# Retrieved experts of a two-block network on one Trainium2 core: u and v rows fetched by one gather from a joined table, dots and mixing in one pass, top-k head by head

## What is computed

```
# per block of 128 tokens (there are two); 8 heads, 128 keys in each of two halves, 16384 experts
q = (hb @ w_q).reshape(tb, 8, 2, 128)
scores = einsum("thpc,hpnc->thpn", q, keys)
s_top, i_top = top_k(scores, 16)                    # 16 best of 128, per head and half
cand = s_top[..., 0, :, None] + s_top[..., 1, None, :]   # 256 sums per head
best, pos = top_k(cand, 16)                         # 16 best of 256
idx = the two key numbers of pos, as 128 * i + j    # 128 experts per token
gate = softmax(best)
u = take(expert_u, idx)                             # [token, 128, 1024]
act = gelu(einsum("tkd,td->tk", u, hb))
vv = take(expert_v, idx)
out = einsum("tk,tkd->td", gate * act, vv)
```

## Time and profile before

| what | us |
|---|---|
| median of 3 timed runs | 3087.06 (3086.28 to 3093.58) |
| span of the profiled execution, first to last instruction | 3081.3 |
| PE / DVE / ACT / POOL busy in it | 2539.9 / 1885.4 / 1017.9 / 549.8 |
| first gather issued, last gather issued | 2268.65, 3058.88 |

### The profile page before, as it was taken

The page is one execution under the profiler, slowest core; times in us unless marked ns, Lnnn a source line. Parts: engine busy times, 40 slices in busy tenths (PEclk is TensorE's granted clock), DMA queues, the critical chain, the costliest instruction groups (busy, mean ns, idle before and its releaser), DMA issues.

```text
span 3081.3 us, 31757 instructions
## 1 busy us (share of the span) xinstructions
PE 2539.9 (82%) x11382; PEld 1991.5 (65%) x11382; DVE 1885.4 (61%) x2532; ACT 1017.9 (33%) x952; POOL 549.8 (18%) x664
## 2 busy tenths in 40 slices
PE   8998999999899999999999979899950067800687
PEld 7777998767788888888888868688850023300233
DVE  5333544431798898888888853534188875388422
ACT  2212331111577686676766731115010000000000
POOL 0000000000000000000000000000036667666775
PEclk9999999999899999999999989999975589955899
DMA  6323554430699999999999953134339998899997
GB/s 220 132 88 96 185 172 154 137 109 25 249 355 353 334 369 338 354 350 338 353 352 333 374 210 118 65 110 172 116 133 370 358 338 302 322 372 364 343 332 266
DMA packets 316765, 775.01 MB, mean 252 GB/s; under 512 B 17850, under 2 KB 59528, under 8 KB 316680
## 3 DMA queue, kind: packets, MB, share of 16 engines
q1 hardware_dynamic: 240996, 503.54, 46.0%
q0 software_dynamic: 73728, 268.47, 24.0%
q10 hardware_dynamic: 1956, 1.86, 0.2%
HBM read 772.76 MB, written 1.05 MB: 251 GB/s over the span
## 4 chain that ended last, share of the span: by engine, by line
PE 73%; POOL 10%; issue 8%; DVE 5%; DMA 2%; ACT 1%; POOLq 1%; DVEq 0%; ACTq 0%
PE banks L498 15%; PE banks L659 12%; PE banks L661 12%; PE banks L660 12%; POOL dense_weights L1236 9%; PE banks L546 5%; PE banks L1007 3%; PE banks L622 2%; PE banks L626 2%; PE banks L459 2%; DMA dense_weights<-in_peer_v,gather_stage 2%; POOL gather_stage L1229 1%; PE banks L816 1%; PE banks L745 1%; PE banks L772 1%
## 5 line engine op out<-in xcount | busy, mean ns | idle before, releaser
L1894 DVE TENSOR_TENSOR expert_tiles_low<-expert_tiles,expert_tiles_high 128x2048 fp32r<-128x2048 f32 x336 | 752.5, 2284 | 90.0 <-ACT expert_tiles_high L1447 89.8
L1007 PE MATMUL banks<-dense_weights,work 128*128 128x512 f32 x768 | 351.0, 614 | 413.7 <-DVE work L2246 206.9
L1447 ACT ACTIVATE expert_tiles_high<-expert_tiles 128x2048 fp32r<-128x2048 f32 x336 | 624.6, 1911 | 66.4 <-DMA expert_tiles<-in_moe_w_down 52.7
L1007 PEld LDWEIGHTS banks<-dense_weights,work 128*128 128x128 f32 x768 | 147.7, 197 | 615.8 <-issue 606.1
L659 PE MATMUL banks<-expert_tiles_high,gathered_parts 128*128 128x512 f32 x896 | 355.4, 397 | 2.2 <-DVE gathered_parts L1903 2.2
L661 PE MATMUL banks<-expert_tiles_high,gathered_parts 128*128 128x512 f32 x896 | 350.5, 391 | 0.0
L660 PE MATMUL banks<-expert_tiles_low,gathered_parts 128*128 128x512 f32 x896 | 349.9, 390 | 0.0
L1209 POOL MEMSET work<- 64x1024 f32 x1 | 0.9, 944 | 1839.4 <-DVE normed L1638 1839.4
L2220 DVE CUSTOM_DVE_ANT_0 dense_weights<-dense_weights,banks 128x1024 f32<-128x1024 f32 x256 | 296.5, 1216 | 50.6 <-DMA dense_weights<-in_peer_u,gather_stage 49.7
L498 PE MATMUL banks<-normed,dense_weights 128*128 128x256 f32 x1280 | 281.3, 382 | 7.1 <-DVE normed L1638 7.1
L1236 POOL DMA_INDIRECT dense_weights<-in_peer_v,gather_stage x256 | 259.5, 1014 | 114.0 <-issue 80.1
(11 more groups left out here) (353 smaller groups left out, 3414.4 us busy)
## 6 DMA issues: line engine op xcount, KB each, us to landing
expert_tiles<-in_moe_w_gate SPq DMA_DIRECT2D x112, 1024.0 KB, 5.1
expert_tiles<-in_moe_w_up SPq DMA_DIRECT2D x112, 1024.0 KB, 5.2
expert_tiles<-in_moe_w_down SPq DMA_DIRECT2D x112, 1024.0 KB, 4.9
dense_weights<-in_w_in SPq DMA_DIRECT2D x12, 2048.0 KB, 7.8
dense_weights<-in_w_xkv SPq DMA_DIRECT2D x8, 2048.0 KB, 8.0
dense_weights<-in_w_in SPq DMA_DIRECT2D x10, 1280.0 KB, 13.8
expert_tiles<-in_ffn_w_gate SPq DMA_DIRECT2D x11, 1024.0 KB, 5.3
expert_tiles<-in_ffn_w_up SPq DMA_DIRECT2D x11, 1024.0 KB, 5.3
```

The source lines that it names most:

```text
L1007: mm = pe.matmul(halves[half], diag[:, q, j, :], gathered_rows[:, q * BATCH + j, half * 512:(half + 1) * 512], start=False, stop=False)
L1447: act.activation(high_tile(j), raw_tile(j), ACT.Copy).then_inc(g.high, 1)
L1894: dve.tensor_tensor(low_tile(j), raw_tile(j), high_tile(j).bitcast(F32), ALU.subtract).then_inc(g.split, 1)
```

## The change

The host hands over one table `peer_rows`, whose row e is u[e] followed by v[e], 8 KB. One gather fetches both rows of a slot (128 rows of 8 KB, 1.05 MB), so there are 256 gathers and not 512. A batch is now two slots (2.1 MB, as before), and there are seven batch buffers: two lie in memory that the first block used, one in the slot of the key weights and four in the slots of the four `pq` weight tiles (`G.pair_at`), and each can be filled when PE is done with what was in it (`G.pair_freed`).

For every batch n of 128, in one pass: DVE makes two dots (`products`), ACT takes gelu of the two, DVE makes two diagonals from `gelu x gate` (`weights`, one tensor_scalar each, run after the dots of the next batch), PE mixes both rows (`mix`, four matmuls of 512 columns) and frees the buffer. DVE's own share of the mixing and the four phases are gone. Top-k is done head by head (`choose`, 16 units), two heads ahead of the gathers, between the batches. POOL reads the indices where they lie, without the staging copy. The loops are written out, not run as loops.

```diff
+PAIR_ROWS = 2
+PAIR_BUFS = 7
+AHEAD_UNITS = 2
+EARLY, LATE = 3, 4
...
+                def mix(b, halves, first, last):
+                    for n in range(b * BLOCK_BATCHES + first, b * BLOCK_BATCHES + last):
+                        pe.wait_ge(diag_ready, n + 1)
...
+                        for j in range(PAIR_ROWS):
+                            for half in range(2):
+                                mm = pe.matmul(halves[half], diag[(n * PAIR_ROWS + j) % 8], pair_rows(n)[:, j, 1, half * 512:(half + 1) * 512],
+                                               start=False, stop=end and j == PAIR_ROWS - 1)
+                        mm.then_inc(mix_done, 1)
...
+                G.pair_at = [RING, RING + 1] + [(keys_at + i) % RING for i in range(RING)]
+                for g in range(4):
+                    linear(("pq", g), "a", 1, x, KT)
+                    scores(0, g)
+                    if g == 0:
+                        tokens("v", 0)
+                    elif g == 1:
+                        first = out_banks("v", 0)
+                    elif g == 2:
+                        mix(0, first, 0, EARLY)
+                G.pair_freed = [None, None] + G.freed[keys_at:]
...
+                mix(0, first, EARLY, BLOCK_BATCHES)
+                second = out_banks("a", 1)
+                mix(1, second, 0, BLOCK_BATCHES)
...
+            for n in range(TB * BLOCK_BATCHES):
+                if n % HEAD_BATCHES == 0:
+                    pool.wait_ge(index_ready, n // HEAD_BATCHES + 1)
+                if n >= PAIR_BUFS:
+                    pool.wait_ge(mix_done, n - PAIR_BUFS + 1)
+                elif G.pair_freed[n]:
+                    pool.wait_ge(*G.pair_freed[n])
+                for j in range(PAIR_ROWS):
...
+                    pool.indirect_dma_start(out=pair_rows(n)[:, j, :, :].rearrange("p t d -> p (t d)"), out_offset=None,
+                                            in_=t["peer_rows"], in_offset=bass.IndirectOffsetOnAxis(ap=rows_at[:, c:c + 1], axis=0)
+                                            ).then_inc(gathered[n % PAIR_BUFS], 16)
...
+                for g in range(4):
                     copies(("pq", g), qP[:, 4 * g:4 * g + 4, :], 2)
...
+                    scores(0, g)
+                    if g == 1:
+                        for u in range(AHEAD_UNITS):
+                            share(u)
+                    elif g == 2:
+                        activations(0, EARLY)
...
+            def choose(u):
+                b, h = divmod(u, PHEADS)
+                dve.wait_ge(act_took, G.took["key_scores", b, h // 2])
+                top16(key_top, key_at, key_scores[b][:, 2 * h:2 * h + 2, :], key_rest, 2)
...
+                def products(n):
+                    dve.wait_ge(gathered[n % PAIR_BUFS], 16 * PAIR_ROWS * (n // PAIR_BUFS + 1))
+                    for j in range(PAIR_ROWS):
+                        u_row, c = pair_rows(n)[:, j, 0, :], n * PAIR_ROWS + j
+                        ins = dve.tensor_tensor_reduce(u_row, u_row, tokens(b), 1.0, 0.0, ALU.mult, ALU.add, dots[:, c:c + 1])
+                    ins.then_inc(dot_done, 1)
...
+                def weights(n):
+                    dve.wait_ge(act_ready, n + 1)
+                    if n >= 4:
+                        dve.wait_ge(mix_done, n - 3)
+                    for j in range(PAIR_ROWS):
+                        c = n * PAIR_ROWS + j
+                        ins = dve.tensor_scalar(diag[c % 8], ident[:, :], acts[:, c:c + 1], gates[:, c // TOPK, c % TOPK:c % TOPK + 1],
+                                                ALU.mult, ALU.mult)
+                    ins.then_inc(diag_ready, 1)
...
+                for u in range(AHEAD_UNITS):
+                    choose(u)
+                for n in range(TB * BLOCK_BATCHES):
+                    u, part = divmod(n, HEAD_BATCHES)
+                    products(n)
+                    if n:
+                        weights(n - 1)
+                    if part == 0:
+                        normalise(u)
+                    elif part == HEAD_BATCHES // 2 - 1 and u + AHEAD_UNITS < UNITS:
+                        choose(u + AHEAD_UNITS)
```

More of the change, by code:

```diff
@@ L337, in two_blocks @@
[L337 to L351, removed]
+        key_scores = [view(6144 + 2048 * b, 2 * PHEADS, PK) for b in range(TB)]
+        diag = [view(10240 + P * i, P) for i in range(8)]
+        key_rest, pairs_, pairs_rest = view(11264, 2, PK), view(11520, 1, TOPK * TOPK), view(11776, 1, TOPK * TOPK)
@@ L1010, in peer @@
-                    pe.wait_ge(zero_ready, 1)
-                    for half in range(2):
-                        G.end(pe.matmul(halves[half], ones[0:1, :], zero_row, start=False, stop=True), ("out", b, half))
+                    return halves
+                def mix(b, halves, first, last):
+                    for n in range(b * BLOCK_BATCHES + first, b * BLOCK_BATCHES + last):
+                        pe.wait_ge(diag_ready, n + 1)
+                        end = n == (b + 1) * BLOCK_BATCHES - 1
+                        for j in range(PAIR_ROWS):
+                            for half in range(2):
+                                mm = pe.matmul(halves[half], diag[(n * PAIR_ROWS + j) % 8], pair_rows(n)[:, j, 1, half * 512:(half + 1) * 512],
+                                               start=False, stop=end and j == PAIR_ROWS - 1)
+                        mm.then_inc(mix_done, 1)
@@ L1582, in scores, with share, activations @@
                     ready(("key_scores", b, g))
[L1583 to L1592 removed]
+                    take(act.activation(key_scores[b][:, 4 * g:4 * g + 4, :], pair(banks_of(("key_scores", b, g)), 4, P), ACT.Copy))
+                def share(u):
+                    act.wait_ge(margin_ready, u + 1)
+                    act.activation(gates[:, u, :], gates[:, u, :], ACT.Exp, accum_out=gate_sum[:, u:u + 1]).then_inc(margin_exp, 1)
+                def activations(first, last):
+                    for n in range(first, last):
+                        act.wait_ge(dot_done, n + 1)
+                        s = slice(n * PAIR_ROWS, (n + 1) * PAIR_ROWS)
+                        act.activation(acts[:, s], dots[:, s], ACT.Gelu).then_inc(act_ready, 1)
+                        if n % HEAD_BATCHES == HEAD_BATCHES - 2 and n // HEAD_BATCHES + AHEAD_UNITS < UNITS:
+                            share(n // HEAD_BATCHES + AHEAD_UNITS)
                 def final(b):
[L1595 to L1596 removed]
+                    act.wait_ge(mix_done, (b + 1) * BLOCK_BATCHES)
+                    n = (0 if b == 0 else 4) + (G.took["out", b, 0] - 1) % 4
+                    step.now(act.activation(final_sq, psum_all[:, n:n + 2, :].rearrange("p h d -> p (h d)"), ACT.Square,
+                                            accum_out=final_ss[:, b:b + 1]))
                     act.activation(final_std[:, b:b + 1], final_ss[:, b:b + 1], ACT.Sqrt, bias=EPS_AP, scale=1.0 / D).then_inc(final_std_ready, 1)
@@ L2265, in finish @@
                 def finish(b):
[L2267 to L2270 removed]
+                    dve.wait_ge(mix_done, (b + 1) * BLOCK_BATCHES)
+                    n = (0 if b == 0 else 4) + (G.took["out", b, 0] - 1) % 4
                     dve.wait_ge(final_std_ready, b + 1)
@@ L2316 @@
     arrays, t = {}, {}
-    for name, a in inputs.items():
+    rows = _np.concatenate([inputs["peer_u_2"][0], inputs["peer_v_2"][0]], axis=1)
+    laid = {name: a for name, a in inputs.items() if name not in ("peer_u_2", "peer_v_2")} | {"peer_rows": rows}
+    for name, a in laid.items():
         a = _np.ascontiguousarray(a)
```

273 lines of the change are left out of this document (66 added, 207 removed).

## The result

The changed kernel takes 2934.43 us (median of 4 runs, 2931.72 to 2938.63), the kernel before 3089.63 us on the same chip (3086.28 to 3093.58). The ratio is 0.949, with a 95% interval of 0.948 to 0.951: 155 us less. 3006 us was forecast, with a range from 2965 to 3060.

What follows compares the result with a forecast made beforehand. DMA was taken to bound the gather stream, with POOL's pace almost on top. Batch 6 at 2288.1, plus 2.2, 695.4 and 14.8, gave a span of 3000.5, 80.8 less than before: 3006 us, range 2965 to 3060.

Steps and rivals of the forecast that it cites:

- The pace of DMA: Steady gather stream: DMA's own pace read as 375 GB/s in the dot phase, 358 in mixing; 5.70 us per batch taken.
- the rival built on it: Gather stream: 8 KB rows flow faster, at 401 GB/s or 5.23 us a batch, giving 2949 us; chance 7%.
- start of `pq` to the gather of batch 6: Kernel start: batch 6 waits for the fourth query tile behind `pq` group 3, which was to end at 2288.1.
- latency: Fixed latency of a gather, beyond its own bytes: between 0 and 4.1 us, taken as 2.2 us.
- 122 batches: Steady stream after the start's gap: 122 batches at 5.70 us each, 695.4 us.
- release to end: After the last landing: last dots, gelu, diagonals, PE mixing, root, scaling and store, 14.8 us.
- the 5.8 that the forecast added: Final sum: the median before, 3087.06 us, lay 5.8 above its span of 3081.3, turning span into time.
- POOL left the bound: POOL's issue: two gathers per batch cost 2.5 us, or 5.0 if doubled, both under 5.69, leaving the pace to DMA.
- The start: Before the steady stream: first gather near 2235.4, 33 us earlier, then DMA idles some 16 us until 2288.1.
- DVE and PE stayed below their limits: Steady stream: DVE has 31.4 us of work per 45.6 us head, 69%; PE 3.6 us per 5.70 us batch, 63%.
- The rival of the mixing phase: Gather stream: 333 GB/s stays as DMA's answer to PE and DVE reading beside it, 6.30 us a batch, 3080 us; 8%.
- The tail: End of the kernel after the last landing: 14.8 us forecast with one PE mixing of 3.7, against 16.0 before.

Runs made afterwards that it cites:

- e9: Changed kernel with fourteen small index copies on POOL ahead of each batch, gathers reading the staged copy: 3045.48 us, ratio 0.986.
- e5: Gathers alone, no network computed, in stages of 4, 8, 16 and 2 KB rows, run once: rows of 4 KB flow at 410 GB/s.
- e4: Kernel before the change with POOL's loop unrolled and the index copy with its wait removed: 3061.68 us, ratio 0.992.
- e3: Changed kernel with no batch mixed on PE ahead of `pq` group 3 (EARLY, LATE = 0, 4 for 3, 4): 2926.17 us, ratio 0.947.
- e7: e1 with a small index copy on POOL and a wait on a constant put back before each batch: 2951.64 us, ratio 0.955.
- e1: Changed kernel with u and v in two tables, two gathers of 4 KB rows per slot, no index copy: 3042.96 us, ratio 0.986.
- e2: Changed kernel with the joined table kept but read by two gathers of 4 KB rows per slot: 3034.99 us, ratio 0.983.
- e10: e1 with gathers reading a staged copy of sixteen index columns, made once a head: 3048.84 us, ratio 0.987.
- e12: e1 with POOL waiting for the landing of batch n-2 before issuing batch n: 3039.67 us, ratio 0.986.
- e11: e1 with four pair buffers in place of seven: 3165.97 us, ratio 1.026.
- e6: Gathers alone with a chain of 2600 dependent small DVE copies beside them, run once: 160 to 165 copies in each 40 us inside a stage.

## Why the prediction was off

**The pace of DMA: the step that failed.** "The engines' own pace is the flow at full share: 368 / 0.98 = 375 GB/s in the dot phase." It is not. I had the right view beside it: POOL's timeline with a batch each 5.69 us, 368.6 GB/s, waiting for no engine. When one limit explains a rate to the third digit, a second "almost on top" needs evidence of its own, and a share of busy time is none: e9 shows 0.96 at 351 GB/s and the changed kernel 1.01 at 419, with the same packets. POOL's issue set the flow of the dot phases; e5 gives 410 GB/s for its rows, and e4, which only drops the copy and unrolls POOL's loop, has 405 in them until POOL stops for another reason. I had even shown 401 GB/s in the earlier trace rows, and gave the rival built on it 7%, "the share of 0.98 speaks against it". The trace of before could give 401 at least as the pace of 4 KB rows: 5.23 us and 2949 us, off by 15.

The Trainium skill (DMA: Bandwidth & Descriptors, "Where 436 GB/s comes from") has HBM bind loads near 358 GB/s per core; the 417 to 420 GB/s over 600 us of this one core do not agree. The same page, "Measured", names that figure as a core's part when two cores that share the memory stream at once, which no run here tries. It has 425 GB/s for 16 MB moved by one core alone, and this the runs bear out: 422 with 8 KB rows, 428 with 16 KB.

**The sum, term by term**, from the start of `pq`, as this execution came to it 7.5 us later than that of before (2217.14 and 2209.68) before anything changed had begun. That is chance: the other kernels with the same first part come to it between 2209.25 and 2217.89.

| term | forecast | measured | difference |
|---|---|---|---|
| start of `pq` to the gather of batch 6 | 78.4 | 79.4 | +1.0 |
| latency (taken as forecast) | 2.2 | 2.2 | |
| 122 batches | 695.4 (5.70 each) | 613.7 (5.03) | -81.7 |
| last bytes to release of the last batch | 0 | 6.9 | +6.9 |
| release to end | 14.8 | 17.5 | +2.7 |
| sum | 790.8 | 719.7 | -71.1 |

The 7.5 us of the earlier part bring the span's own difference to -63.7 (2936.8 for 3000.5). The timed median lies 71.6 under the forecast, 8 more. The profiled execution took 2938.63 us itself, 4.2 over the median. And a span is 1.7 to 2.1 us shorter than its own execution in every kernel of the network that has both on record; the 5.8 that the forecast added was 4 us too many, as the span of before was set against the median of other executions. The measured tail, 9.6 us longer than forecast in two terms, hid a part of the error in the pace.

**What held.** POOL: an 8 KB gather costs what a 4 KB one does, and POOL left the bound. The start was right as a chain: top-k of one head took 9.3 us (2233.7 to 2243.0), the first gather went at +26.3 from `pq` (+25.7 forecast), the gap in the stream is there (share 0.09 in 2280:2300), and e3 confirms its cause: without the three mixing batches batch 6 goes 15.4 us sooner. DVE and PE stayed below their limits, at 77% and 75% busy against 69% and 63% forecast, of a batch that is 12% shorter than I thought; PE's clock was 0.87 to 0.91. Diagonals take 0.28 us each (1.11 for four in the timeline above), 0.22 forecast. The rival of the mixing phase did not happen: 333 GB/s was not DMA's answer to PE and DVE, 419 flow beside both.

**What was missed besides.** The tail: I added one batch's mixing, but the order on DVE (weights one batch behind the dots) makes it two. And the 6.9 us in which one DMA engine finishes alone.

**Where the 155 us come from.** e9 keeps all of the change but POOL's pace, and gains 43 us. The earlier start and the end of separate mixing phases are in these; no run parts them. The other 111 are POOL's pace. Of these, the changed kernel takes 17 less than e7, whose batches POOL offers in 5.16 us. Of the 17 some 11 are the row's length (5.12 us a batch at e5's 410 GB/s against 5.03, 122 times, an estimate). The rest of the 111 would have come in the one-pass kernel from 4 KB rows too, if POOL issued a batch in 5.16 us as in e7. Without the copy 4 KB rows do not give it: e1 has the stops, and takes 3043 us.

## What to carry to other kernels

Before a share of busy DMA is called a limit, look at who issues: if an engine's issue pitch gives the measured rate and it waits for nobody, the rate is its own, and the DMA engines' true pace has to be looked for in a stretch with a backlog or measured alone. For gathers issued by GpSimd the price is per gather and not per byte (0.94 + 0.30 us for 128 rows of 2 to 16 KB), so the longer row is worth most where it takes the issuing engine off the path. Buffers lent by weights tie the stream's start to the matmuls that release them: what is done ahead of those matmuls costs the stream, even if PE looks free for it.

## What was not expected of the hardware

- **Busy share and rate come apart.** 0.96 at 351 GB/s, 0.98 at 368 and at 380, 1.01 at 419, 1.03 at 410. An 8 KB packet lasts 282 ns in a full stream and 316 ns in one offered at the slower pace.
- **One DMA engine lags.** After a long full stream one of sixteen engines goes on alone: for 6.9 us in the changed kernel (share 0.06 from 2913 on), for some 5 us in e3 (0.18, 0.06, 0.05 in windows of 2 us from 2900 to 2906, release at 2906.07), for about 1 us in the slower e9 (0.31, 0.06, 0.00 in windows of 1 us from 3027 to 3030, release at 3029.38). In the kernel before the share fell from 0.82 to 0.08 from one window of 1 us to the next (3063 to 3065), its last landing at 3065.3. That it is one engine is read from the share of 0.06; the views do not name engines. A batch is released by its slowest engine, so the last landing comes later than bytes over rate says.
- **Engines stop, mostly together,** for up to 5.8 us on POOL when 4 KB gathers are issued without a copy in each batch, in five kernels (e1, e2, e4, e10, e12), and neither in e7 nor with 8 KB rows. With four buffers (e11) POOL has one such wait, of 1.2 us. It costs some 90 us (e1 against e7). It needs more than the gathers (e5, e6 have none). The cause is open.
- **A staged index copy cost 0.20 + 0.27 us in e7**, with POOL's loop written out and a wait on a constant, against 0.19 + 0.81 in the loop of before, which waits on a register's value and adds to a semaphore behind each wait. Which of these makes the 0.54 us no run parts.
